# Head of a one-core transformer block: where the first transfers are issued, and a wait per pass in the first eight k tiles

## The chip, the cores and the metric

The kernel runs on one core of a Trainium2 chip. The metric is the device time of one execution in microseconds (us). Three executions of the kernel before took 547.81, 547.93 and 548.54 us: a median of 547.93.

## The reference

One layer of a hybrid streaming encoder on x of 256 tokens x 2048 features, all in float32. The part that matters here is the beginning:

```python
h = rms_norm(x, norm_gain[l])                      # x * rsqrt(mean(x*x)) * gain
proj = jnp.einsum('btd,de->bte', h, w_in[l])       # 2048 -> 9296 columns
qa, ka, va, ga, qb, kb, vb, gb, qi, ki, wi = jnp.split(proj, offsets, axis=-1)
...                                                # two attentions, gates
x = x + jnp.einsum('bte,ed->btd', y, w_out[l])     # 2048 -> 2048
return rms_norm(x, final_gain)
```

The kernel applies the gain before the matmuls and the row factor rsqrt(mean) after them, so the first projection can begin before the norm is known.

## The kernel before, in words

**The work.** Every projection is computed in column blocks of 512 with the contraction over 2048 features cut into 16 k tiles of 128. float32 accuracy is had from a faster matmul type with three passes: each operand is split into a rounded part (hi) and the rest (lo), and the product is a_hi*w_hi + a_hi*w_lo + a_lo*w_hi, each pass once per half of the 256 tokens (m = 0, 1). So one k tile of a token block is six matmuls of 512 columns. The activations are split once, at the head (acts holds a_hi and a_lo), the weights as they stream in.

**The weight stream.** A unit is two k tiles, 512 KB. Units go through a ring of four buffers (w_raw). SyncE issues the loads; ScalarE makes w_hi (a rounding copy), VectorE makes w_lo = w_raw - w_hi, TensorE multiplies. Each step tells the next by a semaphore: w_landed, hi_done, lo_done, mm_done. SyncE may load unit u when lo_done says that unit u - 4 is split.

**The head.** The first block (va, block 0 of the schedule) shares its time with the arrival of everything. Its first four units (HALVED = 4, u = 0 to 3) are loaded, split and signalled by halves of one k tile each: the first half of unit u under half_landed, half_hi and half_lo, the second under w_landed, hi_done and lo_done. The transposed activations arrive in tiles: xT tile 0 alone, tile 1 alone, then two k tiles at a time, between the weights. In this document w0a and w0b are the two halves of unit 0, w1a the first half of unit 1 (k tile 2), and so on.

- SyncE (lines 268 to 274) issues in this order: w0a, xT tile 1, w0b, xT tiles 2 and 3, w1a, w1b, xT 4 and 5, w2a, ... Units 4 to 7 (lines 275 to 280) are whole transfers, each waiting for lo_done, each followed by two xT tiles. The narrow weights (line 281) and x itself (line 286) come next on the same queue.
- ScalarE's queue issues xT tile 0 (line 663), then loads its function table (664). Its order for the halves (671 to 682) is: a_hi of k tile k (a_part, 667; for k = 1 it waits for the norm weights and for xT), then w_hi of that half (681).
- GpSimd issues the norm weights (gain, line 321: 128 rows of 64 bytes) and rel_bias (322), then fills constants.
- VectorE makes a_hi of k tile 0 itself (922), when the norm weights and xT tile 0 are there; then for each half a_lo (929), w_lo (937). Behind the eighth half it copies in bias_ext (943), which waits for rel_bias.
- TensorE first multiplies zeros (414). k tile 0 is done in three passes, each with its own wait (first_k, 417 to 428). For k tiles 1 to 7 it waits for a_lo and for w_lo, and then does all six matmuls (mm3, lines 429 to 439; mm3's own lines 371 to 373). From unit 4 on the wait is for a whole unit's lo_done (unit, 375 to 384).

After the first block, feature blocks (line 390 on, two matmuls per k tile and 128 columns), the narrow projection (447 to 451, weights nw_hi and nw_lo, split at 699 and 976), the attentions between them, and the output projection at the end.

Of the kernel before, what the change touches and what calls it, by code (L numbers as in the profile page):

```python
# [13 lines left out]
P = 128  # L14
D = 2048
T = 256
TM = T // P
KT = D // P
CB = 512
# [19 lines left out]
UK = 2  # L39
# [5 lines left out]
def hybrid_block(nc, xT, x, norm_gain, w_blocks, w_narrow, rel_bias, wo_blocks, final_gain, out):  # L45
# [7 lines left out]
    with ExitStack() as ctx:  # L53
# [11 lines left out]
        w_hi = sb("w_hi", [P, RING, UK, CB], f32r)  # L65
        w_lo = sb("w_lo", [P, RING, UK, CB], f32r)
# [5 lines left out]
        a_hi, a_lo = acts[:, :, 0, :], acts[:, :, 1, :]  # L72
# [45 lines left out]
        gain = sb("gain", [P, KT])  # L118
# [9 lines left out]
        xT_land = qk[:, :, :].rearrange("p c t -> p (c t)").rearrange("p (k t) -> p k t", k=KT)  # L128

        acc = pb("acc", [P, 4 * CB])  # L130
# [4 lines left out]
        hi_done = sem("hi_done")  # L135
# [4 lines left out]
        xT_landed = [sem(f"xT_landed{c}") for c in range(UNITS)]  # L140
# [116 lines left out]
        def _(sp):  # L257
# [9 lines left out]

            for u in range(HALVED):
                sp.dma_start(w_raw[:, u, 0:CB], w_blocks[VA_FIRST, u, :, 0:CB]).then_inc(half_landed[u], 16)
                if u == 0:  # L270
                    sp.dma_start(xT_land[:, 1, :], xT[:, 1, :]).then_inc(xT_landed[0], 16)
                sp.dma_start(w_raw[:, u, CB:2 * CB], w_blocks[VA_FIRST, u, :, CB:2 * CB]).then_inc(w_landed[u], 16)
                k = slice(UK * (u + 1), UK * (u + 2))
                sp.dma_start(xT_land[:, k, :], xT[:, k, :]).then_inc(xT_landed[u + 1], 16)
# [43 lines left out]

        @block.gpsimd
        def _(pool):  # L320
            pool.dma_start(gain[:, :], norm_gain).then_inc(gain_landed, 16)
            pool.dma_start(bias_ext[:, 0:2 * MAX_REL + 1], rel_bias).then_inc(row_landed, 16)
            nc.gpsimd.memset(ident[:, :], 0.0).then_inc(cleared, 1)
            nc.gpsimd.memset(ones[:, :], 1.0).then_inc(cleared, 1)
# [42 lines left out]
        def _(pe):  # L367
            def mm3(dst, k, m, hi, lo, start, stop):

                t = slice(m * P, m * P + P)  # L370
                nc.tensor.matmul(dst, a_hi[:, k, t], hi, start=start, stop=False)  # L371
                nc.tensor.matmul(dst, a_hi[:, k, t], lo, start=False, stop=False)  # L372
                return nc.tensor.matmul(dst, a_lo[:, k, t], hi, start=False, stop=stop)  # L373
# [40 lines left out]
                nc.tensor.matmul(acc[:, m * CB:m * CB + CB - HD // 2], ki_bd[:, 0, 0:P], zeros,  # L414
                                 start=True, stop=True)

            def first_k(a, w, start):
                for m in range(TM):
                    nc.tensor.matmul(acc[:, m * CB:m * CB + CB], a[:, 0, m * P:m * P + P], w[:, 0, 0, :],
                                     start=start, stop=False)  # L420

            pe.wait_ge(a0_done, 1)
            pe.wait_ge(half_hi, 1)
            first_k(a_hi, w_hi, True)
            pe.wait_ge(alo_done, 1)
            first_k(a_lo, w_hi, False)
            pe.wait_ge(half_lo, 1)
            first_k(a_hi, w_lo, False)
            for u in range(HALVED):
                for kk in range(UK):  # L430
                    k = u * UK + kk
                    if k == 0:
                        continue
                    pe.wait_ge(alo_done, k + 1)
                    pe.wait_ge((half_lo, lo_done)[kk], u + 1)
                    for m in range(TM):
                        last = mm3(acc[:, m * CB:m * CB + CB], k, m, w_hi[:, u, kk, :], w_lo[:, u, kk, :],
                                   False, False)
                last.then_inc(mm_done, 1)
            for u in range(HALVED, UNITS):  # L440
                pe.wait_ge(alo_done, UK * u + UK)
# [196 lines left out]
        def _(act):  # L638
# [15 lines left out]
            def features_low(g, half, first):  # L654
# [5 lines left out]
                parts = acc[:, 2 * pair * CB:2 * pair * CB + 2 * CB].rearrange("p (f x t) -> p f x t", f=2, x=2)  # L660
                nc.scalar.activation(low[:, half, :, :], parts[:, :, 1, :], ACT.Copy).then_inc(low_out, 1)  # L661

            act.dma_start(xT_land[:, 0, :], xT[:, 0, :]).then_inc(xT0_landed, 16)
            nc.scalar.preload_act_table(ACT.Exp)

            def a_part(k):
# [655 lines left out]
```

## Time and profile before

| | |
|---|---|
| runs shown, median (lowest, highest) | 547.93 us (547.81, 548.54) |
| the profiled execution's own time | 547.97 us |
| its span, first to last instruction | 546.2 us |
| mean granted clock of TensorE | 0.998 of full speed |
| TensorE busy | 535.4 us, 98% |
| VectorE busy | 332.0 us, 61% |
| ScalarE busy | 259.3 us, 47% |
| GpSimd busy | 17.1 us, 3% |
| moved by DMA | 103.73 MB, mean 190 GB/s |

The profile comes from one execution. Its span lies inside the execution's own time. Engines are PE (TensorE matmuls), PEld (its weight loads), DVE (VectorE), ACT (ScalarE), POOL (GpSimd) and SP (SyncE); a q behind the name is the sequencer that issues transfers. A busy share is an average over the whole span: where the time can change is read from idle stretches of the engine that ends last and from what ended them.

### The profile page before, as it was taken

The numbers are of one execution on the slowest core, as the hardware profiler recorded it, in microseconds if no ns is written. First come the engines' busy times: TensorE is split into PE (matmuls) and PEld (weight loads), VectorE is DVE, ScalarE is ACT, GpSimd is POOL, SyncE is SP. The second block draws the span as 40 slices with busy tenths as digits, with TensorE's granted clock in tenths as the row PEclk, the third lists the DMA queues.
The fourth block names the chain that finished last, engine by engine and source line by source line (L and its number), as shares of the span: only waits on it lengthen the run. The fifth ranks groups of instructions, "written<-read, shape, count | busy, mean of one in ns | idle before, by whom it ended". The sixth has DMA issues, their size and how long they took to land.

```text
span 546.2 us, 8107 instructions
## 1 busy us (share of the span) xinstructions
PE 535.4 (98%) x2780; PEld 454.7 (83%) x2780; DVE 332.0 (61%) x488; ACT 259.3 (47%) x364; POOL 17.1 (3%) x31
## 2 busy tenths in 40 slices
PE   7999999999999999999999999999999999999994
PEld 4889888888888888888888888888888888888883
DVE  5855564656566565567655657556674757556464
ACT  6883544444444443444554545354445445444342
POOL 1002020202000000000000000000000000000000
PEclk9999999999999999999999999999999999999999
DMA  8987655557555656665555554554555566565613
GB/s 289 394 290 241 189 168 182 168 170 237 185 174 174 199 193 189 191 193 162 181 160 167 173 157 158 184 164 157 181 168 172 159 218 217 188 199 184 211 57 154
DMA packets 59909, 103.73 MB, mean 190 GB/s; under 512 B 3280, under 2 KB 44656, under 8 KB 59376
## 3 DMA queue, kind: packets, MB, share of 16 engines
q1 hardware_dynamic: 58944, 98.78, 55.5%
q0 software_dynamic: 656, 4.22, 2.4%
q10 hardware_dynamic: 288, 0.46, 0.2%
q8 instruction: 12, 0.20, 0.2%
q14 instruction: 9, 0.07, 0.0%
HBM read 101.34 MB, written 2.11 MB: 189 GB/s over the span
## 4 chain that ended last, share of the span: by engine, by line
PE 97%; DMA 1%; DVE 1%; ACT 0%; SPq 0%; issue 0%; DVEq 0%; ACTq 0%
PE acc L404 27%; PE acc L371 16%; PE acc L373 16%; PE acc L372 16%; PE acc L402 13%; PE aux L546 1%; PE aux L522 1%; DMA w_raw<-w_blocks 1%; PE aux L449 1%; PE aux L484 1%; PE acc L407 1%; PE aux L550 1%; PE aux L525 1%; PE aux L535 1%; PE aux L486 1%; PE aux L605 0%
## 5 line engine op out<-in xcount | busy, mean ns | idle before, releaser
L896 DVE TENSOR_TENSOR w_lo<-w_raw,w_hi 128x1024 fp32r<-128x1024 f32 x172 | 212.3, 1236 | 187.4 <-ACT w_hi L646 186.8
L646 ACT ACTIVATE w_hi<-w_raw 128x1024 fp32r<-128x1024 f32 x172 | 182.0, 1059 | 242.5 <-PE acc L404 123.3
L404 PE MATMUL acc<-acts,w_hi 128*128 128x512 f32 x640 | 224.3, 396 | 0.0
L402 PE MATMUL acc<-acts,w_lo 128*128 128x256 f32 x600 | 168.8, 281 | 0.0
L371 PE MATMUL acc<-w_hi,acts 128*128 128x512 f32 x382 | 150.5, 394 | 1.8 <-DVE w_lo L937 1.5
L373 PE MATMUL acc<-w_hi,acts 128*128 128x512 f32 x382 | 149.0, 390 | 0.0
L372 PE MATMUL acc<-w_lo,acts 128*128 128x512 f32 x382 | 148.7, 389 | 0.0
L404 PEld LDWEIGHTS acc<-acts,w_hi 128*128 128x128 f32 x640 | 119.1, 188 | 26.1
L402 PEld LDWEIGHTS acc<-acts,w_lo 128*128 128x128 f32 x600 | 113.1, 189 | 0.8
L371 PEld LDWEIGHTS acc<-w_hi,acts 128*128 128x128 f32 x382 | 71.8, 188 | 17.1 <-issue 2.8
L373 PEld LDWEIGHTS acc<-w_hi,acts 128*128 128x128 f32 x382 | 71.7, 188 | 15.2
L372 PEld LDWEIGHTS acc<-w_lo,acts 128*128 128x128 f32 x382 | 71.8, 188 | 14.4
L860 ACT ACTIVATE t_gate<-z 128x512 f32<-128x512 f32 x8 | 5.0, 627 | 15.3 <-DVE z L1246 15.3
L661 ACT ACTIVATE low<-acc 128x512 f32<-128x512 f32 x20 | 11.6, 581 | 0.0
L407 PE MATMUL acc<-acts,w_lo 128*128 128x256 f32 x40 | 11.2, 281 | 0.0
L1027 DVE SCALAR_TENSOR_TENSOR iscore<-relu,w_idx,iscore 128x256 f32<-128x256 f32 (+1 forms) x32 | 11.2, 413 | 0.0
L910 DVE TENSOR_TENSOR qk<-acc,low 128x512 f32<-128x512 f32 (+1 forms) x16 | 10.9, 684 | 0.0
L363 POOL DMA_DIRECT2D v<-x x1 | 0.5, 531 | 317.7 <-PE aux L550 317.7
L840 ACT ACTIVATE acts<-aux 128x512 fp32r<-128x512 f32 x8 | 4.7, 605 | 9.4 <-PE aux L605 9.4
L777 ACT ACTIVATE p<-p,neg_top,q_rate 128x256 f32<-128x256 f32 (+1 forms) x16 | 8.5, 535 | 1.0 <-DVE neg_top L1130 1.0
L546 PEld LDWEIGHTS aux<-v,pT 128*128 128x128 f32 x64 | 8.4, 191 | 0.5
L546 PE MATMUL aux<-v,pT 128*128 (+1 forms) x64 | 8.4, 275 | 0.0
(137 smaller groups left out, 306.9 us busy)
## 6 DMA issues: line engine op xcount, KB each, us to landing
w_raw<-w_blocks SPq DMA_DIRECT2D x140, 512.0 KB, 3.6
w_raw<-wo_blocks SPq DMA_DIRECT2D x32, 512.0 KB, 3.4
w_raw<-w_blocks SPq DMA_DIRECT2D x8, 256.0 KB, 6.3
v<-x SPq DMA_DIRECT2D x2, 1024.0 KB, 9.4
v<-x POOLq DMA_DIRECT2D x1, 2048.0 KB, 8.7
qk<-xT SPq DMA_DIRECT2D x7, 256.0 KB, 6.5
o<-ext_dram POOLq DMA_DIRECT2D x1, 1024.0 KB, 6.9
fgain<-final_gain POOLq DMA_DIRECT2D x1, 1024.0 KB, 7.5
```

The costliest lines, as they stand in the source:

```text
L371: nc.tensor.matmul(dst, a_hi[:, k, t], hi, start=start, stop=False)
L372: nc.tensor.matmul(dst, a_hi[:, k, t], lo, start=False, stop=False)
L373: return nc.tensor.matmul(dst, a_lo[:, k, t], hi, start=False, stop=stop)
L402: nc.tensor.matmul(acc[:, bank:bank + T], w_lo4[:, u % RING, q, c], a_hi[:, k, :], start=False, stop=False)
L404: last = nc.tensor.matmul(whole, w_hi4[:, u % RING, q, c], acts[:, k, :, :], start=(k == 0), stop=(k == KT - 1))
L407: nc.tensor.matmul(acc[:, bank:bank + T], w_lo4[:, u % RING, q, c], a_hi[:, k, :], start=False, stop=False)
L546: nc.tensor.matmul(aux[3][:, h * HD:h * HD + HD], pT1[:, h, kt, :], v_flat[:, ds(place(pair, kt) + h * HD, HD)], start=(kt == 0), stop=(kt ...
L646: nc.scalar.activation(flat(w_hi[:, s, :, :]), w_raw[:, s, :], ACT.Copy).then_inc(hi_done, 1)
L661: nc.scalar.activation(low[:, half, :, :], parts[:, :, 1, :], ACT.Copy).then_inc(low_out, 1)
L896: nc.vector.tensor_tensor(flat(w_lo[:, s, :, :]), w_raw[:, s, :], flat(w_hi[:, s, :, :]).bitcast(f32), ALU.subtract).then_inc(lo_done, 1)
L910: nc.vector.tensor_tensor(dst, parts[:, :, 0, :], low[:, half, :, :], ALU.add).then_inc(feat_out, 1)
L1027: last = nc.vector.scalar_tensor_tensor(total[:, :], relu[:, h, :], w_idx[:, 1 - t, 4 * i + 2 * c + h:4 * i + 2 * c + h + 1], total[:, :], ...
```

## The change

It moves three issues and cuts one wait. xT tile 1 goes from SyncE's queue to ScalarE's, the norm weights from GpSimd's to ScalarE's; ScalarE then issues norm weights, xT tile 0, xT tile 1, in this order, ahead of its table load. On SyncE w0a and w0b are then the first two. In the first eight k tiles TensorE does three passes per k tile in the order a_hi*w_hi, a_lo*w_hi, a_hi*w_lo, with a wait before each: for w_hi and a_hi, for a_lo, for w_lo. first_k is replaced by early_pass; the number of matmuls is the same. Units 4 to 7 and everything behind them stay.

```diff
--- before.py
+++ after.py
@@ -267,8 +267,6 @@
 
             for u in range(HALVED):
                 sp.dma_start(w_raw[:, u, 0:CB], w_blocks[VA_FIRST, u, :, 0:CB]).then_inc(half_landed[u], 16)
-                if u == 0:
-                    sp.dma_start(xT_land[:, 1, :], xT[:, 1, :]).then_inc(xT_landed[0], 16)
                 sp.dma_start(w_raw[:, u, CB:2 * CB], w_blocks[VA_FIRST, u, :, CB:2 * CB]).then_inc(w_landed[u], 16)
                 k = slice(UK * (u + 1), UK * (u + 2))
                 sp.dma_start(xT_land[:, k, :], xT[:, k, :]).then_inc(xT_landed[u + 1], 16)
@@ -318,7 +316,6 @@
 
         @block.gpsimd
         def _(pool):
-            pool.dma_start(gain[:, :], norm_gain).then_inc(gain_landed, 16)
             pool.dma_start(bias_ext[:, 0:2 * MAX_REL + 1], rel_bias).then_inc(row_landed, 16)
             nc.gpsimd.memset(ident[:, :], 0.0).then_inc(cleared, 1)
             nc.gpsimd.memset(ones[:, :], 1.0).then_inc(cleared, 1)
@@ -414,28 +411,25 @@
                 nc.tensor.matmul(acc[:, m * CB:m * CB + CB - HD // 2], ki_bd[:, 0, 0:P], zeros,
                                  start=True, stop=True)
 
-            def first_k(a, w, start):
+            def early_pass(a, w, k, start=False):
                 for m in range(TM):
-                    nc.tensor.matmul(acc[:, m * CB:m * CB + CB], a[:, 0, m * P:m * P + P], w[:, 0, 0, :],
-                                     start=start, stop=False)
-
-            pe.wait_ge(a0_done, 1)
-            pe.wait_ge(half_hi, 1)
-            first_k(a_hi, w_hi, True)
-            pe.wait_ge(alo_done, 1)
-            first_k(a_lo, w_hi, False)
-            pe.wait_ge(half_lo, 1)
-            first_k(a_hi, w_lo, False)
+                    last = nc.tensor.matmul(acc[:, m * CB:m * CB + CB], a[:, k, m * P:m * P + P],
+                                            w[:, k // UK, k % UK, :], start=start, stop=False)
+                return last
+
             for u in range(HALVED):
                 for kk in range(UK):
                     k = u * UK + kk
+                    pe.wait_ge((half_hi, hi_done)[kk], u + 1)
                     if k == 0:
-                        continue
+                        pe.wait_ge(a0_done, 1)
+                    else:
+                        pe.wait_ge(ahi_done, k)
+                    early_pass(a_hi, w_hi, k, start=(k == 0))
                     pe.wait_ge(alo_done, k + 1)
+                    early_pass(a_lo, w_hi, k)
                     pe.wait_ge((half_lo, lo_done)[kk], u + 1)
-                    for m in range(TM):
-                        last = mm3(acc[:, m * CB:m * CB + CB], k, m, w_hi[:, u, kk, :], w_lo[:, u, kk, :],
-                                   False, False)
+                    last = early_pass(a_hi, w_lo, k)
                 last.then_inc(mm_done, 1)
             for u in range(HALVED, UNITS):
                 pe.wait_ge(alo_done, UK * u + UK)
@@ -660,7 +654,9 @@
                 parts = acc[:, 2 * pair * CB:2 * pair * CB + 2 * CB].rearrange("p (f x t) -> p f x t", f=2, x=2)
                 nc.scalar.activation(low[:, half, :, :], parts[:, :, 1, :], ACT.Copy).then_inc(low_out, 1)
 
+            act.dma_start(gain[:, :], norm_gain).then_inc(gain_landed, 16)
             act.dma_start(xT_land[:, 0, :], xT[:, 0, :]).then_inc(xT0_landed, 16)
+            act.dma_start(xT_land[:, 1, :], xT[:, 1, :]).then_inc(xT_landed[0], 16)
             nc.scalar.preload_act_table(ACT.Exp)
 
             def a_part(k):
```

## Rows read from the trace of the kernel before

**Rows 1.** the page: TensorE's busy line, and the chain's shares by engine

```profile
PE 535.4 (98%) x2780; PEld 454.7 (83%) x2780; DVE 332.0 (61%) x488; ACT 259.3 (47%) x364; POOL 17.1 (3%) x31
...
PE 97%; DMA 1%; DVE 1%; ACT 0%; SPq 0%; issue 0%; DVEq 0%; ACTq 0%
```

**Rows 2.** timeline of TensorE: start us, us, instruction [idle before <-releaser]

```profile
8.10 0.47 PE L371 MATMUL acc<-w_hi,acts 128*128 128x512 f32 x1 [1.12 <-DVE w_lo L937]
...
10.08 0.47 PE L371 MATMUL acc<-w_hi,acts 128*128 128x512 f32 x1 [0.35 <-DVE w_lo L937]
...
11.09 0.39 PE L372 MATMUL acc<-w_lo,acts 128*128 128x512 f32 x1
...
449.71 0.47 PE L371 MATMUL acc<-w_hi,acts 128*128 128x512 f32 x1 [0.36 <-DVE acts L1227]
```

**Rows 3.** windows: us, busy (x) of each engine, clock, DMA share, GB/s

```profile
12.00:538.90 526.90, 526.54 (x2757) 450.02 (x2755) 322.96 (x470) 250.64 (x349) 14.41 (x12) 1.00 0.58 188
```

**Rows 4.** the chain that ended last, up to k tile 2: start, us, what

```profile
2.61 5.94 DMA w_raw<-w_blocks
8.58 0.64 ACT w_hi L681
9.24 0.70 DVE w_lo L937
```

**Rows 5.** timeline of VectorE, k tiles 2 and 3

```profile
8.49 0.48 DVE L929 SCALAR_TENSOR_TENSOR acts<-qk,gain,acts 128x256 fp32r<-128x256 f32 x1 [0.54 <-ACT acts L667]
...
10.25 0.68 DVE L937 TENSOR_TENSOR w_lo<-w_raw,w_hi 128x512 fp32r<-128x512 f32 x1
```

**Rows 6.** DMA issues of the first 2 us: KB each, us to landing

```profile
qk<-xT ACTq DMA_DIRECT2D x1, 128.0 KB, 3.6
```

**Rows 7.** timeline of the head: issues, table load, first halves

```profile
0.75 0.42 ACTq L663 DMA_DIRECT2D qk<-xT  x1
...
1.20 0.42 SPq L271 DMA_DIRECT2D qk<-xT  x1
1.20 1.28 ACT L664 ACT_TABLE_LOAD   x1 [1.20 <-PEq L1315]
1.25 0.68 POOL L321 DMA_DIRECT2D gain<-norm_gain  x1 [0.79 <-POOLq L1315]
...
4.20 0.63 ACT L681 ACTIVATE w_hi<-w_raw 128x512 fp32r<-128x512 f32 x1 [1.72 <-DMA w_raw<-w_blocks]
...
4.72 0.35 DVE L922 TENSOR_SCALAR acts<-qk,gain 128x256 fp32r<-128x256 f32 x1 [3.31 <-DMA gain<-norm_gain]
```

**Rows 8.** windows from 4 to 10, columns as in rows 3

```profile
4.00:6.00 2.00, 1.69 (x6) 0.60 (x4) 1.24 (x3) 1.03 (x2) 0.00 (x0) 1.00 0.85 242
6.00:8.00 2.00, 0.98 (x4) 0.30 (x2) 1.29 (x3) 0.68 (x2) 0.00 (x0) 1.00 0.98 318
8.00:10.00 2.00, 1.63 (x6) 1.05 (x6) 1.24 (x3) 1.88 (x4) 0.00 (x0) 1.00 1.05 402
```

**Rows 9.** timeline around unit 4

```profile
15.28 1.06 ACT L646 ACTIVATE w_hi<-w_raw 128x1024 fp32r<-128x1024 f32 x1 [0.29 <-DMA w_raw<-w_blocks]
...
16.37 1.23 DVE L896 TENSOR_TENSOR w_lo<-w_raw,w_hi 128x1024 fp32r<-128x1024 f32 x1 [0.47 <-ACT w_hi L646]
...
18.36 0.39 PE L371 MATMUL acc<-w_hi,acts 128*128 128x512 f32 x1
```

**Rows 10.** timeline around the narrow weights

```profile
37.85 1.47 DVE L976 TENSOR_TENSOR nw_lo<-nw_raw,nw_hi 128x1280 fp32r<-128x1280 f32 x1
...
40.52 0.40 PE L449 MATMUL aux<-acts,nw_hi 128*80 128x256 f32 x2
```

**Rows 11.** DMA queues over 0 to 40 us: packets, MB, share

```profile
q10 hardware_dynamic: 144, 0.13, 0.9%
q0 software_dynamic: 96, 0.03, 0.4%
```

**Rows 12.** window behind the last matmul, columns as in rows 3

```profile
542.00:544.00 2.00, 0.00 (x0) 0.00 (x0) 0.23 (x1) 0.00 (x0) 0.00 (x0) 1.00 0.83 313
```

## The prediction

> **What bounds the kernel now.** I read the page first. TensorE is busy 98% of the 546.2 us span, and 97% of the chain that ended last is TensorE [rows 1]. Nothing in the diff removes a matmul, so the change can only shorten time in which TensorE stands still, and only at the head, where the diff works. TensorE's own timeline shows how much there is [rows 2]: it has 1.12 us of idle before k tile 1 (8.10) and 0.35 before k tile 2 (10.08). Behind that it is busy in 526.5 of the 526.9 us from 12 to 538.9 [rows 3]; the one gap, 0.36 at 449.71, waits for VectorE's y tiles, which TensorE itself feeds, so it moves with the rest [rows 2]. The only number that can move the end is therefore the time at which the unbroken run of matmuls begins, 10.08, provided that what comes after can keep up with an earlier start.
>
> The chain that ended last says what sets 10.08 [rows 4]: the first half of the second weight unit (w1a) is issued on SyncE at 2.61 and its landing comes 5.94 us later, at 8.55; ScalarE rounds it to w_hi (8.58 to 9.21), VectorE makes w_lo (9.24 to 9.93), and TensorE starts 0.15 us later. Its activations are there before: a_lo, made from a_hi, starts at 8.49 and ends at 8.97 [rows 5]. The 5.94 us are not latency of one transfer. The first xT tile, issued at 0.75 to empty engines, took 3.6 us [rows 6]. The DMA engines are 85, 98 and 105% busy in the stretches from 4 to 10 [rows 8], so w1a waits for the bytes ahead of it.
>
> **The change part by part.** *A wait per pass* (eight k tiles). Before, k tile 2 waited for a_lo and w_lo, then ran six matmuls. Now its first two, a_hi with w_hi, need only w_hi (9.21) and a_hi. With the same 0.15 us from an operand's end to the matmul, they start at 9.36, 0.72 earlier. The fifth matmul of a k tile starts 1.01 after its first (11.09 against 10.08 [rows 2]), so the third pass is due at 10.37; w_lo is usable at 9.93 + 0.15 = 10.08, so the third pass finds it ready and there is no new gap. For later k tiles TensorE needs 1.38 us each ((18.36 - 10.08) / 6, [rows 2, 9]), while VectorE starts the next w_lo 1.01 after this one (9.24, 10.25 [rows 4, 5]), so the cover grows. The extra waits (three per k tile for two) stand in TensorE's sequencer, ahead of the array: free here, since the run has matmuls queued. If that cover went, the price would be 0.15 for one. Same matmuls, another order: their price stays at 1.38 / 6 = 0.23.
>
> *What is late next.* Unit 4, the first with whole 512 KB transfers, keeps the old wait. Its weights reach ScalarE at 15.28 (that engine was idle 0.29 for the DMA), w_lo starts at 16.37 and ends at 17.60, so TensorE can start at 17.75 at the earliest; it starts at 18.36 now [rows 9]. The slack is 0.61, under the 0.72. So of the 0.72 only 0.61 gets through, the rest becomes a 0.1 us gap at unit 4. Units 5 to 7 gain cover: VectorE needs 2 x 0.48 + 1.23 = 2.19 for a unit [rows 5, 9], TensorE 2 x 1.38. The next tight place is the narrow weights: their w_lo ends at 37.85 + 1.47 = 39.32 and TensorE takes it up at 40.52, a slack of 1.05 with the 0.15 off [rows 10], more than 0.61. So k tiles 2 to 7 and unit 4 both go by the DMA stream, and every shift of that stream, D, moves both: gain = min(0.72, 0.61) - D.
>
> *k tile 1, both halves first on SyncE.* The 128 KB xT tile leaves SyncE's queue, so every later issue there is one issue slot, 0.47 us, earlier (SyncE's second issue is at 1.20, its fifth at 2.61: [rows 4, 7]). Its w0b now lands between 4.8 (its new issue at 1.20 plus 3.6) and, if nothing is won, 1.5 us before k tile 1's start at 8.10, that is 6.6 (0.63 for w_hi, 0.69 for w_lo and the hand-over). Either way its w_hi is there by 7.3 and k tile 1 is over by 8.8, before 9.36. It is off the path: the 1.12 us of idle shrinks and the idle before k tile 2 grows by as much. For w1a the 0.47 is worth nothing as long as the DMA engines are full: the same bytes stand ahead of it (two weight halves, xT0 and xT1 with 128 KB each, now both on ScalarE's queue, and the double tile of k 2 and 3). Were ScalarE's queue served beside SyncE's with engines of its own, w1a would land up to 0.47 earlier and the sum would be 547.0. The Trainium skill, page "DMA: Bandwidth & Descriptors", section "Issuing engines are not separate DMA queues", says that all issuers share the same 16 engines and only issue time is saved; by that rule the term is zero, and the full engines agree.
>
> *ScalarE's queue and norm weights.* ScalarE now issues three transfers instead of one: 2 x 0.42 us more before its table load (1.28 long, [rows 7]), so that ends at 3.3 instead of 2.48. The first w_hi starts at 4.20, so 0.9 of cover is left. Were it gone, only k tile 0 would move, which is off the path. xT0 is issued 0.45 later and lands about 4.8 rather than 4.35; the norm weights leave at 0.75 instead of 1.25 and land before the 4.72 that they set now; a_hi of k tile 0 comes within 0.2 of the present 4.72 [rows 6, 7]. xT1, behind xT0 and beside w0b, lands at 5 to 5.6 instead of 4.7; ScalarE needs it before w_hi of k tile 1: off the path. GpSimd loses 0.68 us of issue and sends rel_bias that much sooner; what uses it comes on VectorE behind the eighth w_lo half, which the chain has not reached by 10.25, so nothing waits for it.
>
> *Price of the small packets.* The norm weights are 128 rows of 64 B. No row shows such rows on a hardware queue. On GpSimd's queue the whole head's 96 small packets took 0.4% of 16 x 40 us, 27 ns each; on ScalarE's queue 144 packets (128 of 1 KB and 16 completion writes) took 0.9%, 40 ns each [rows 11]. With their 16 completion writes the new rows cost 144 x 27 = 3.9 us over 16 engines = 0.24 us, less 0.05 for the 32 packets that leave GpSimd's queue: +0.19. The ends are 0 (they are issued first of all, when the engines have nothing else) and 0.36 (40 ns). I take 0.19, by the row of small packets. The Trainium skill, page "DMA: Bandwidth & Descriptors", section "Why small descriptors are slow (HBM only)", charges a fixed overhead per packet, which points the same way; no row here shows it for 64 B.
>
> *The shortfall.* From 4 to 8 the engines moved 242 and 318 GB/s, from 8 to 10 402, though busy [rows 8]. The lacking 0.49 MB are 1.2 us at 402. GpSimd's queue sends its two small transfers in these microseconds; whether it is the cause can't be read. If the shortfall goes, D falls by 1.2; if it doubles, D rises by 1.2. I take it as it is, since most of its bytes come after the moved pieces.
>
> **Sum.** D = +0.19, gain 0.61 - 0.19 = 0.42. The profiled execution took 547.97 (span 546.2 and 1.8 around it), 0.04 over the median of 547.93: 547.97 - 0.42 = 547.55, called 547.5. About 0.2% (1.1 us) is what a measurement can tell from no change.
>
> **The rivals.**
> - *The shortfall vanishes* (faster). For it: it ends soon after GpSimd's two small transfers, and one of them is taken off that queue. Against: low rates last to 7, and rel_bias stays there. Gives 547.5 - 1.2 = 546.3, or 546.9 if half goes. Chance 0.18 for enough of it to pass the 0.2%.
> - *The clock falls in the new idle* (slower). k tile 1 may be over at 7.7 to 8.8 with k tile 2 at 9.36: one idle stretch of up to 1.6 us, where 1.12 and 0.35 stood. If TensorE went to 1.2 GHz there, each k tile would take 1.38 more; between one and two tiles long, this costs some 2 us: 549.5. It decides as soon as it takes more than 0.42, two matmuls' worth. Against: the granted clock is 1.00 through the idle of before (6 to 10, [rows 8]), and after the last matmul, with no work for TensorE from 539 on, the window 542 to 544 still has 1.00 [rows 12]. Chance 0.04.
> - *The shortfall deepens*, two hardware queues taking turns for longer: D = +1.2 more, 548.7 at full size, slower than before from D = 0.61. Chance 0.10, of which 0.04 beyond the 0.2%.
> - *Nothing changes*: w_hi and a_hi aren't what ends last, or unit 4 gives all back: 547.9. Chance 0.08.
> - My forecast: 0.60, own range 547.1 to 547.9.
>
> Faster by over 0.2%: 0.18. Slower: 0.08. Within: 0.74. The range leaves out the full clock case and the last of the vanished shortfall: 546.4 to 548.4.
>
> **What would show it.** In the timeline of the changed kernel k tile 2's first pass starts right behind its w_hi, at about 9.4 to 9.6; the unbroken run starts there; ScalarE's wait for unit 4 is at 15.3 to 15.5, and a TensorE gap of about 0.1 stands at 17.8 to 18.0; the granted clock stays 1.00. The windows 4 to 8 keep their 240 and 320 GB/s. I am wrong if w1a's w_hi starts before 8.1 or after 9.3, if unit 4's moves by over 0.5, or if TensorE shows a new gap behind 20.

## The result and the profile after

The changed kernel takes 548.54 us (median of 22 runs, 547.61 to 550.37), the kernel before 547.72 in the same comparison (22 runs, 547.17 to 548.65). The ratio is 1.0018, 95% interval 1.0011 to 1.0024: slower by some 0.8 us, little, but the interval is clear of 1. The forecast was 547.5 in a range of 546.4 to 548.4: wrong in sign, and the time lies just outside. Ratios and intervals, here and below, are taken over the executions and are not quotients of the two medians printed beside them; they leave out two executions that lie far off, 1094.31 us of the kernel before and 670.88 of e3's.

The profiled execution took 548.76, with a span of 547.0. Of the changed kernel's page, the lines that answer to [rows 1] and the line of ScalarE's queue:

```profile
PE 536.9 (98%) x2780; PEld 456.3 (83%) x2780; DVE 331.6 (61%) x488; ACT 259.1 (47%) x364; POOL 16.6 (3%) x30
...
q10 hardware_dynamic: 576, 0.60, 0.3%
...
PE 97%; DMA 1%; ACT 0%; DVE 0%; ACTq 0%; issue 0%; DVEq 0%
```

The same matmuls are busy 1.5 us longer than before (536.9 against 535.4): a first hint that some ran slower. From 12 us on nothing has changed. This window answers to [rows 3]: TensorE again lacks 0.36 us in the whole stretch.

```profile
12.00:539.70 527.70, 527.34 (x2761) 450.62 (x2759) 323.18 (x471) 250.99 (x349) 14.46 (x12) 1.00 0.57 188
```

So the loss is at the head. The timeline of the changed kernel there (start us, us, instruction, idle before and what ended it), beside [rows 2, 4, 5, 7]; line 416 is the new early_pass, x4 and x2 are merged matmuls:

```profile
5.10 0.35 DVE L918 TENSOR_SCALAR acts<-qk,gain 128x256 fp32r<-128x256 f32 x1 [3.68 <-DMA qk<-xT]
...
5.60 2.05 PE L416 MATMUL acc<-w_hi,acts 128*128 128x512 f32 x4 [0.77 <-DVE acts L918]
...
7.65 0.51 ACT L663 ACTIVATE acts<-qk,gain 128x256 fp32r<-128x256 f32 x1 [3.22 <-DMA qk<-xT]
8.07 0.61 ACT L677 ACTIVATE w_hi<-w_raw 128x512 fp32r<-128x512 f32 x1
...
8.73 1.94 PE L416 MATMUL acc<-w_hi,acts 128*128 128x512 f32 x4 [0.24 <-ACT w_hi L677]
...
10.52 0.63 PE L416 MATMUL acc<-w_lo,acts 128*128 128x512 f32 x2
...
10.98 1.08 PE L416 MATMUL acc<-w_hi,acts 128*128 128x512 f32 x4
...
12.36 0.84 PE L416 MATMUL acc<-w_hi,acts 128*128 128x512 f32 x3
```

Two things are to be seen. First, ScalarE stands idle for 3.22 us until xT tile 1 has landed, and only then makes a_hi and w_hi of k tile 1, so that TensorE starts k tile 1 at 8.73 instead of 8.10. Second, its first four matmuls take 1.94 us; k tile 2's take 1.08. They are 0.43 apart, twice the 0.23 of the rest: TensorE ran at the lower of its two levels, 1.2 GHz, until about 10.4. The chain that ended last starts with the same transfer, where before it started with w1a:

```profile
0.75 0.42 ACTq L657
1.21 0.45 ACTq L658
1.68 5.88 DMA qk<-xT
7.65 0.51 ACT acts L663
8.16 0.53 ACT w_hi L677
8.73 10.58 PE acc L416 x42
```

The windows of the DMA engines, as in [rows 8]:

```profile
4.00:6.00 2.00, 1.23 (x3) 0.43 (x2) 0.87 (x3) 0.43 (x1) 0.00 (x0) 1.00 0.92 206
6.00:8.00 2.00, 2.00 (x6) 1.39 (x5) 0.57 (x1) 0.35 (x1) 0.00 (x0) 1.00 1.04 351
8.00:10.00 2.00, 1.76 (x5) 1.07 (x4) 1.77 (x4) 2.00 (x6) 0.00 (x0) 1.00 1.06 408
```

The low rate is still there, a little earlier. The clock column reads 1.00 here, although the matmuls in it are 0.43 apart: ahead of the first change that a profile records, this column says nothing. It was one of my arguments against the clock.

Of the signs that the prediction named for being wrong, none came: w1a's w_hi started at 8.99, unit 4's at 14.92 (0.36 earlier), and no gap stands behind 20. What did show it is the first pass of k tile 2, at 10.98 and not at 9.4 to 9.6.

### The profile page after: what moved, and what is told of

Same layout as the page of the kernel before. It is cut to its first block, busy times and chain, and to the rows that moved or that the text cites. A ratio compares the mean times of both kernels' runs of the same rounds, so it can differ in the third digit from the quotient of the medians.

```text
span 547.0 us, 8107 instructions
## 1 busy us (share of the span) xinstructions
PE 536.9 (98%) x2780; PEld 456.3 (83%) x2780; DVE 331.6 (61%) x488; ACT 259.1 (47%) x364; POOL 16.6 (3%) x30
## 4 chain that ended last, share of the span: by engine, by line
PE 97%; DMA 1%; ACT 0%; DVE 0%; ACTq 0%; issue 0%; DVEq 0%
PE acc L401 27%; PE acc L368 15%; PE acc L370 15%; PE acc L369 15%; PE acc L399 13%; PE acc L416 2%; PE aux L540 1%; PE aux L516 1%; DMA qk<-xT 1%; PE aux L443 1%; PE aux L478 1%; PE acc L404 1%; PE aux L544 1%; PE aux L519 1%; PE aux L529 1%; PE aux L480 1%
## 5 line engine op out<-in xcount | busy, mean ns | idle before, releaser
L369 PE MATMUL acc<-w_lo,acts 128*128 128x512 f32 x368 | 143.2, 389 | 0.0
L370 PEld LDWEIGHTS acc<-w_hi,acts 128*128 128x128 f32 x368 | 69.1, 188 | 14.8
L368 PEld LDWEIGHTS acc<-w_hi,acts 128*128 128x128 f32 x368 | 69.1, 188 | 14.3 <-issue 0.6
L369 PEld LDWEIGHTS acc<-w_lo,acts 128*128 128x128 f32 x368 | 69.1, 188 | 13.8
L416 PE MATMUL acc<-w_hi,acts 128*128 128x512 f32 x32 | 10.4, 455 | 1.0 <-DVE acts L918 0.8
L416 PEld LDWEIGHTS acc<-w_hi,acts 128*128 128x128 f32 x32 | 6.8, 221 | 4.4 <-issue 2.1
```

Of the source, the lines that this page charges most:

```text
L416: last = nc.tensor.matmul(acc[:, m * CB:m * CB + CB], a[:, k, m * P:m * P + P], w[:, k // UK, k % UK, :], start=start, stop=False)
```

## The experiments

Three theories: Q, the transfer order (xT1 is late and ScalarE takes its a_hi ahead of w_hi); C, the clock; and, as a rival, that waits or passes themselves cost something. Kernels measured together share their runs of the kernel before, so its median differs a little below (547.40 to 547.65).

### e1 and e1b: the waits per pass alone

All transfers as before; in TensorE's program first_k and the loop behind it are replaced:

```diff
-            def first_k(a, w, start):
+            def early_pass(a, w, k, start=False):
...
-                    for m in range(TM):
-                        last = mm3(acc[:, m * CB:m * CB + CB], k, m, w_hi[:, u, kk, :], w_lo[:, u, kk, :],
-                                   False, False)
+                    last = early_pass(a_hi, w_lo, k)
```

> The kernel before with the three waits per k tile alone; all transfers are issued as before. Theory Q (the loss comes from the transfer order: xT tile 1 on ScalarE's queue lands at 7.56 instead of 4.5, and ScalarE takes its a_hi ahead of w_hi of k tile 1): no loss here, k tile 2 starts behind its w_hi at 9.4, time 0.3 to 0.6 us under the kernel before. Theory C (the loss comes from TensorE's clock, which the changed kernel's profile shows at its lower level until 10.40 and the old one's at its upper level from 4.72): the same here if the rise needs what TensorE does before 5.1, since that is unchanged; so also no loss. Theory W (the waits themselves or the new order of passes cost something): slower than before by 0.3 or more.

> The kernel of e1 once more, on the same chip as e14, to compare the two and to settle whether the waits per pass alone are faster than the kernel before: 0.2 to 0.5 us under it, at the floor of 547.2 in most executions; its trace has the narrow matmuls 0.2 to 0.4 us behind the end of their w_lo.

Measured: 547.32 against 547.64 (ratio 0.9998, 0.9989 to 1.0007), and again 547.12 against 547.54 (0.9997, 0.9987 to 1.0006). The medians are 0.3 and 0.4 lower, but both intervals hold 1: the waits do no harm, and their gain can't be told from none. Theory W falls. The trace of e1b shows a head much faster than that of [rows 2], and where the gain goes (timeline):

```profile
7.50 1.07 PE L419 MATMUL acc<-w_hi,acts 128*128 128x512 f32 x4
...
8.86 1.07 PE L419 MATMUL acc<-w_hi,acts 128*128 128x512 f32 x4
...
10.22 1.07 PE L419 MATMUL acc<-w_hi,acts 128*128 128x512 f32 x4
...
36.20 0.40 PE L404 MATMUL acc<-acts,w_hi 128*128 128x512 f32 x1
36.80 0.39 PE L402 MATMUL acc<-acts,w_lo 128*128 128x256 f32 x1 [0.21 <-DVE w_lo L893]
...
39.49 0.39 PE L404 MATMUL acc<-acts,w_hi 128*128 128x512 f32 x1
39.73 0.40 PE L446 MATMUL aux<-acts,nw_hi 128*80 128x256 f32 x2
```

k tile 3 starts at 10.22; in the trace of [rows 2] it starts at 11.54, 1.32 later. The same two feature matmuls in the trace of the kernel before:

```profile
37.46 0.40 PE L404 MATMUL acc<-acts,w_hi 128*128 128x512 f32 x1
37.69 0.28 PE L402 MATMUL acc<-acts,w_lo 128*128 128x256 f32 x1
```

So e1b is still 1.26 ahead at 36.20 (37.46 before), and 0.89 at 36.80, where TensorE waits for the w_lo of a feature unit; the first matmuls behind the wait cost another 0.1. The narrow matmuls then start at 39.73, 0.79 earlier than in [rows 10]. They follow the end of their own w_lo (37.98 + 1.47 = 39.45) by 0.28, as expected, but they did not wait for it: they start 0.24 behind the matmul at 39.49, the ordinary distance. The chain of e1b says what holds that feature unit (start, us, what):

```profile
21.22 11.30 DMA v<-x
...
34.54 0.96 ACT w_hi L643
35.53 1.24 DVE w_lo L893
...
36.80 0.39 PE acc L402
```

It is x itself, 11.3 us on its way. ScalarE squares each half of x for the norm (1.9 us) before it makes w_hi of this unit, so everything behind waits for x to land. In the trace of e1 the same place takes its lead from 0.96 to 0.77.

### e2: the moved transfers alone

The changed kernel with TensorE's old waits.

> The changed kernel with the old waits of TensorE (six matmuls of a k tile behind a_lo and w_lo): the three moved transfers alone. Theory Q: k tile 1 has to wait for w_lo, about 9.4 + 0.15 = 9.55, instead of w_hi, 8.73; k tile 2 follows at 10.9 at the upper clock against 10.08 before: 0.8 us slower than the kernel before, even with the clock up, and about as slow as or slower than the changed kernel. Theory C: slower only by what the lower clock takes, 0.8 to 2 us, and the profile shows matmuls 0.43 us apart at 8 to 10.

Measured: 551.53 (550.79 to 551.69) against 547.64, ratio 1.0064 (1.0051 to 1.0078): 3.9 us slower, more than either theory said. xT tiles on ScalarE's queue took 5.5 us at the median; its k tile 1 starts at

```profile
10.61 0.77 PE L368 MATMUL acc<-w_hi,acts 128*128 128x512 f32 x1 [2.00 <-DVE w_lo L936]
...
11.17 0.63 PE L369 MATMUL acc<-w_lo,acts 128*128 128x512 f32 x1
...
11.60 0.63 PE L370 MATMUL acc<-w_hi,acts 128*128 128x512 f32 x1
```

after 2.0 us of idle, with matmuls 0.43 apart. So the transfers are the harmful half of the change, and the waits per pass buy some 3 us of it back. How much of these 3 us is the clock can't be told from one trace: in it xT1 landed later (8.6) than in any trace of the changed kernel, and matmuls stayed 0.43 apart until 14.2.

### e3: xT tile 1 back on SyncE's queue

```diff
                 sp.dma_start(w_raw[:, u, 0:CB], w_blocks[VA_FIRST, u, :, 0:CB]).then_inc(half_landed[u], 16)
+                if u == 0:
+                    sp.dma_start(xT_land[:, 1, :], xT[:, 1, :]).then_inc(xT_landed[0], 16)
...
-            act.dma_start(xT_land[:, 1, :], xT[:, 1, :]).then_inc(xT_landed[0], 16)
```

> The changed kernel with xT tile 1 back on SyncE's queue behind the first half weights; norm weights and xT tile 0 stay on ScalarE's queue, the waits per pass stay. Theory Q: xT1 lands at 4.5 to 5 again, k tile 1 starts at 6.5 to 7.3, k tile 2 behind its w_hi at 9.0 to 9.4: 0.5 to 1 us faster than the kernel before. Theory C: k tile 0 still starts late (xT0 behind the norm weights, 5.5 instead of 5.1), the clock stays low until past 8 in most executions, but since the run of matmuls begins with k tile 2 at 9.4 the lower clock costs only what is left of it: between 0.5 faster and 0.5 slower than the kernel before.

Measured: 547.64 against 547.64, ratio 0.9997 (0.9987 to 1.0006). With the one moved issue put back, the loss is gone. Its trace has xT1 landing 3.4 us after its issue; k tile 1 starts at 7.77, 2 at 9.27, 3 at 10.67. The 0.5 to 1 us under the kernel before that theory Q promised did not come; the time lies in theory C's range, but the late clock that C expected isn't in the trace either (the first four matmuls of k tile 0 take 1.17). This execution took 548.25: 0.7 ahead of the kernel before until 36 us, it lost 1.0 in a gap at 37.92, at the same feature unit as in e1b, where x landed at 33.6 and not 32.5.

### e6 and e10: what stands ahead on ScalarE's queue

e6 has the norm weights back on GpSimd's queue, e10 issues them last. e10's edit:

```diff
-            act.dma_start(gain[:, :], norm_gain).then_inc(gain_landed, 16)
             act.dma_start(xT_land[:, 0, :], xT[:, 0, :]).then_inc(xT0_landed, 16)
             act.dma_start(xT_land[:, 1, :], xT[:, 1, :]).then_inc(xT_landed[0], 16)
+            act.dma_start(gain[:, :], norm_gain).then_inc(gain_landed, 16)
```

> The changed kernel with the norm weights back on GpSimd's queue; xT tiles 0 and 1 stay on ScalarE's. Theory G (the 128 small rows ahead of xT0 and xT1 cost ScalarE's queue a turn each, beside a 2 KB packet of SyncE's queue): xT0 lands near 4.3 again and xT1 0.7 or more earlier than 7.56; the time falls by 0.5 us or more against the changed kernel. Theory X (xT1 is late because it stands on a second queue, behind xT0 and beside the bytes of SyncE's queue while the rate is low from 4 to 7): xT1 lands at 6.8 or later all the same, ScalarE's w_hi of k tile 1 starts at 7.4 or later, and the time stays within 0.4 us of the changed kernel.

> The changed kernel with ScalarE's three transfers in the order xT0, xT1, norm weights. Theory G (xT1 is late because it stands behind the 128 small rows): xT0 lands near 4.4, xT1 near 5.4 as in e6, and now it is the norm weights that are late, 5.5 to 7; k tile 0 then starts at 6 or later, k tile 1's w_hi at 7.4 to 8.1, and the time stays between the kernel before and the changed one. Theory X2 (ScalarE's queue as such is served late): xT1 lands at 6.8 or later in this order too, and the time is the changed kernel's or above.

Measured: e6 548.24 against 547.65 (1.0004, 0.9994 to 1.0013); e10 549.63 against 547.40 (1.0044, 1.0031 to 1.0057). DMA issues of the first 2 us, e6 and then e10 (KB each, median us to landing):

```profile
qk<-xT ACTq DMA_DIRECT2D x2, 128.0 KB, 3.9
...
gain<-norm_gain POOLq DMA_DIRECT2D x1, 8.0 KB, 4.3
```

```profile
qk<-xT ACTq DMA_DIRECT2D x2, 128.0 KB, 3.9
...
gain<-norm_gain ACTq DMA_DIRECT2D x1, 8.0 KB, 5.2
```

With nothing ahead, both xT tiles land in time (xT1 at 5.4 in both); X and X2 fall. The loss of e6 can't be told from none, though its median is 0.6 above: in its trace k tile 0 waits for the norm weights until 5.6 and runs at the lower clock. But G isn't shown either: e6 gained 0.3 on the changed kernel and not 0.5, e10 is slower than the changed kernel, and in e10 the norm weights, 8 KB, take 5.2 us as third transfer, where xT1, 128 KB, took 5.9 as third in the changed kernel. What they share is the slot, issued at 1.68, and what stands beside it: SyncE's third transfer, the 256 KB of xT 2 and 3, issued 0.01 earlier. In the changed kernel's list of issues it took 5.7 us:

```profile
qk<-xT SPq DMA_DIRECT2D x1, 256.0 KB, 5.7
```

and landed at 7.38, xT1 at 7.56; in e10 it landed at 6.69, the norm weights at 6.90. Whether the small rows ahead add to xT1's delay is left open. e10 also loses because k tile 0 waits for the norm weights, 2.77 us of idle, and in its trace the clock falls to 0.50 at 7.76 and comes back at 11.17.

### e4, e8, e13: filling TensorE's idle

The changed kernel with more zero matmuls, before k tile 0 (e4; e8 is the same for a second trace), and in e13 between k tiles 0 and 1 as well. e13's edit (e4 has the first line only):

```diff
+            nc.tensor.matmul(acc[:, 0:192], ki_bd[:, 0, 0:P], zeros[:, 0:192], start=True, stop=True)
...
+                    if k == 0:
+                        for m in (0, 1, 0):
+                            nc.tensor.matmul(acc[:, m * CB:m * CB + 192], ki_bd[:, 0, 0:P], zeros[:, 0:192],
+                                             start=False, stop=False)
```

> The changed kernel with one more zero matmul of 192 columns ahead of the first pass, so that TensorE works until about 5.5 and has next to no idle before k tile 0. Nothing else is touched. Theory C (the clock rises late because TensorE stands idle before a later first pass): the clock is up by 7 in the profile, the matmuls of k tile 1 are 0.23 apart, and the time falls by 0.8 us, to that of the kernel before. Theory Q alone: no change against the changed kernel, 0.8 us slower than before. Both together: the time equals the kernel before, as k tile 2 would start at 8.73 + 1.4 = 10.1 with the clock up, just where it stood.

> The same kernel as e4, for a second trace: its times lay at 547.9 and 549.0 but also three times at 550.3 to 550.6, while the one trace, of an execution of 547.91, shows the upper clock from 4.35 on. Theory C2 (the clock rises during the zero matmuls and falls again in the idle of 1.5 us between k tiles 0 and 1, or rises only late): in a slow execution matmuls of k tiles 1 to 3 are 0.43 apart. Theory D (the slow executions come from late transfers): matmuls are 0.23 apart throughout and xT1 or unit 4 lands 2 us later.

> The changed kernel with the longer zero matmuls of e4 and three more zero matmuls of 192 columns between k tiles 0 and 1 (they add zero to the sums), so that TensorE has next to no idle from 1.5 to 8.7 while all transfers are as in the changed kernel. Theory C (what the changed kernel loses beyond the kernel before is TensorE's clock, low for longer because TensorE stands idle before k tile 0 and before k tile 1): the time is 547.4 to 548.0, 0.5 or more under the changed kernel, no execution at 550, and the trace shows the clock up before 8.2 and staying. Theory Q alone (the transfers set it, whatever the clock): within 0.3 of the changed kernel's 548.5 or above.

Measured: e4 550.32 (547.91 to 550.63) against 547.64, ratio 1.0042 (1.0028 to 1.0056); e8's one execution 547.98; e13 548.96 (548.35 to 550.02) against 547.40, ratio 1.0033 (1.0021 to 1.0046). Both traces of e4's kernel have the upper clock from k tile 0 on, start k tile 1 at 8.71 and 8.67 and take 547.91 and 547.98, as expected where transfers and a good clock act together. They are the cleanest pair with the changed kernel's first trace, which starts k tile 1 at the same 8.73 with the lower clock and took 548.76. But the median of e4 is 1.8 above the changed kernel's, which none of the theories expected: the longer zero matmuls are no cure. Its executions of 550.3 to 550.6 have a mean granted clock of 0.992 to 0.994 where that of 547.91 has 0.998, which speaks for C2, a fall in mid-course; I have no trace of one. e13 went against theory C and as theory Q alone says: no time came back. Its trace has the upper clock from 4.8 on and is slow by the transfer alone; xT1 landed at 8.1:

```profile
9.27 1.19 PE L417 MATMUL acc<-w_hi,acts 128*128 128x512 f32 x4 [0.87 <-ACT w_hi L682]
...
10.76 1.09 PE L417 MATMUL acc<-w_hi,acts 128*128 128x512 f32 x4
...
12.14 1.07 PE L417 MATMUL acc<-w_hi,acts 128*128 128x512 f32 x4
```

### e9, e15, e16: three more traces of the changed kernel

> The changed kernel again, for a second trace. If xT1's landing on ScalarE's queue is what holds k tile 1, it lands between 6.8 and 8.6 here too and k tile 1 starts 1.1 us behind it; the time is then 547.6 to 550.4, by the clock in the first 12 us. If the 7.56 of the first trace was chance, it lands before 6 and the time is below 547.6.

> The changed kernel, a third trace. Theory C (clock beside transfers): its time follows from two rows, the start of k tile 1 (8.2 to 8.8, by xT1's landing at 7.0 to 7.6) and the clock: with the upper clock by 8, 547.4 to 548.0; with the lower clock until 10 or later, 548.6 or more. Transfers alone: the time follows k tile 1's start, whatever the clock.

> The changed kernel, a fourth trace; the same expectation as for the third.

Measured, one execution each: 547.51, 549.46 and 550.71. TensorE's timeline of e9, k tiles 1 and 3:

```profile
8.24 1.20 PE L416 MATMUL acc<-w_hi,acts 128*128 128x512 f32 x4 [1.18 <-ACT w_hi L677]
...
11.10 1.07 PE L416 MATMUL acc<-w_hi,acts 128*128 128x512 f32 x4
```

of e15:

```profile
6.84 1.16 PE L416 MATMUL acc<-w_hi,acts 128*128 128x512 f32 x4 [2.02 <-DVE acts L918]
...
8.91 2.08 PE L416 MATMUL acc<-w_hi,acts 128*128 128x512 f32 x4 [0.19 <-ACT w_hi L677]
...
13.08 1.07 PE L416 MATMUL acc<-w_hi,acts 128*128 128x512 f32 x4
```

with its windows (columns as in [rows 3]; the clock is the third number from the end):

```profile
5.00:8.34 3.34, 1.50 (x6) 0.90 (x6) 1.44 (x3) 0.51 (x2) 0.00 (x0) 1.00 0.96 326
8.34:11.75 3.41, 3.22 (x9) 2.26 (x8) 3.35 (x7) 3.41 (x8) 0.00 (x0) 0.50 1.05 399
11.75:14.00 2.25, 2.25 (x12) 1.84 (x11) 2.25 (x6) 2.25 (x6) 0.00 (x0) 1.00 1.05 403
```

and of e16:

```profile
9.63 2.07 PE L416 MATMUL acc<-w_hi,acts 128*128 128x512 f32 x4 [1.36 <-ACT w_hi L677]
...
12.36 1.66 PE L416 MATMUL acc<-w_hi,acts 128*128 128x512 f32 x4
...
14.32 1.08 PE L416 MATMUL acc<-w_hi,acts 128*128 128x512 f32 x4
```

In e15 xT0 landed late too (at 6.2, issued at 1.20), TensorE stood idle for 2.02 us before k tile 0, and the clock, up when k tile 0 ran (four matmuls in 1.16), fell to the lower level for the next microseconds. In e16 it was low until 13.6. xT1 landed at 7.74 and 8.47, and k tile 1 started later than the expectation had it. Both theories act, and they add up. Take e9 as base (k tile 1 at 8.24, k tile 3 at 11.10, 2.86 apart at the upper clock) and shift its time by the start of k tile 3, that is, 536.41 plus that start:

| trace | k tile 1 | k tile 3 | apart | 536.41 + k tile 3 | took |
|---|---|---|---|---|---|
| before | 8.10 | 11.54 | 3.44 | 547.95 | 547.97 |
| changed, first | 8.73 | 12.36 | 3.63 | 548.77 | 548.76 |
| changed, e9 | 8.24 | 11.10 | 2.86 | (base) | 547.51 |
| changed, e15 | 8.91 | 13.08 | 4.17 | 549.49 | 549.46 |
| changed, e16 | 9.63 | 14.32 | 4.69 | 550.73 | 550.71 |
| e13 | 9.27 | 12.14 | 2.87 | 548.55 | 548.55 |
| e10 | 9.82 | 13.22 | 3.40 | 549.63 | 549.65 |
| e1b | 7.50 | 10.22 | 2.72 | 546.63 | 547.13 |

All but e1b agree within 0.03 us; e1b is 0.5 above, which is what the feature unit behind x took back at 36.80. In the changed kernel's four traces xT1 moves k tile 1 by up to 1.39 (8.24 to 9.63), and the clock adds 0, 0.77, 1.31 and 1.83 to the distance of k tiles 1 and 3. (Before, the distance holds 0.35 of idle that the old wait left.)

The lower clock during k tile 0 is not the changed kernel's own. With the transfers as before the first four matmuls of k tile 0 took 2.05 us in e1, 2.00 in e1b and 2.04 in e11. There k tile 1 follows without idle, at 7.50 to 7.70, and its four take 1.07 to 1.09, at the upper clock. In the changed kernel's first trace and in e16 TensorE then stood idle for 0.24 and 1.36 us, waiting for xT1's tile, and the clock stayed low until 10.4 and 13.6.

### e7: rel_bias late

e1's kernel with GpSimd's remaining small transfer moved behind a wait:

```diff
-            pool.dma_start(bias_ext[:, 0:2 * MAX_REL + 1], rel_bias).then_inc(row_landed, 16)
...
+            pool.wait_ge(hi_done, 1)
+            pool.dma_start(bias_ext[:, 0:2 * MAX_REL + 1], rel_bias).then_inc(row_landed, 16)
```

> The kernel of e1 (the kernel before with the waits per pass) with rel_bias issued on GpSimd only behind the second w_hi half (about 7.5) instead of at 1.9. Theory B (GpSimd's transfer of 8 rows of 1028 bytes slows the DMA engines from 4 to 7): the windows 4 to 8 move 350 GB/s and more, w1a's w_hi starts by 8.0, unit 4's w_hi by 14.4, and the time is 0.3 us or more under e1's. Theory N (the low rate has nothing to do with that transfer): windows 4 to 8 stay at 240 to 330 GB/s, and the time is e1's within 0.2 us.

Measured: 547.40 against 547.65, ratio 0.9995 (0.9986 to 1.0003), e1's time. Windows 4 to 8 of e7:

```profile
4.00:6.00 2.00, 1.55 (x4) 0.67 (x3) 1.20 (x3) 1.69 (x3) 0.00 (x0) 1.00 0.92 290
6.00:8.00 2.00, 2.00 (x11) 1.60 (x10) 1.72 (x4) 1.17 (x3) 0.53 (x1) 1.00 0.90 316
```

Theory N: 290 and 316 GB/s, and e1's time. w1a's w_hi did start at 7.34, as theory B has it, but the rate stayed low and unit 4's w_hi started at 15.24. rel_bias isn't the cause of the low rate, and what is stays open.

### e11, e12, e14: looking for a better version

e11 gives units 4 to 7 the same treatment as the head; e12 adds the norm weights on ScalarE's queue behind xT0; e14 is e11 with VectorE's nw_lo ahead of rk_cols and q_unit.

```diff
-                pe.wait_ge(alo_done, UK * u + UK)
-                unit(0, u)
+                pe.wait_ge(hi_done, u + 1)
+                pe.wait_ge(alo_done, UK * u + UK)
+                for part, (a, w) in enumerate(((a_hi, w_hi), (a_lo, w_hi), (a_hi, w_lo))):
+                    if part == 2:
+                        pe.wait_ge(lo_done, u + 1)
...
```

> The kernel of e1 (transfers as before, waits per pass in k tiles 0 to 7) with units 4 to 7 of the first block treated alike: both w_hi passes of a unit behind hi_done, the w_lo pass behind lo_done. Theory U (unit 4's wait for w_lo is the wall that gives the gain of e1 back: its TensorE start is 0.15 behind the end of w_lo in the traces of e1 and e3): unit 4 starts right behind k tile 7 or 0.15 behind w_hi's end, and the time falls by a further 0.3 to 1.0 us, until the next wall. Theory L (a later place, the narrow weights or units 8 to 11 that wait for x, sets the floor of 547.0 to 547.2 that all faster kernels share): the time stays e1's within 0.2 us.

> The kernel of e11 with the norm weights on ScalarE's queue behind xT0, and xT1 on SyncE's queue as before. If the norm weights' way over GpSimd's queue (landing at 4.6 to 5.6 in the traces) costs anything, k tile 0 starts at 4.9 to 5.1 steadily and the clock is up earlier more often: 0 to 0.4 us under e11. If the small rows beside the first weight halves cost more than that, 0.2 or more above e11.

> The kernel of e11 with VectorE's nw_lo (1.47 us) moved ahead of rk_cols and q_unit, which nothing needs before 57 us. Theory L (the faster kernels share a floor because the narrow weights' w_lo ends at 39.3 to 39.5 in all of them and TensorE starts on it 0.27 behind): nw_lo ends near 38.9, the narrow matmuls start at 39.2, and the time is 0.3 to 0.5 us under e11 and e1, so 546.8 to 547.1. If the head alone (the first 18 us) set the time: as e11, 547.3 to 547.5.

Measured: e11 547.47 against 547.40 (1.0000, 0.9991 to 1.0008), e12 547.70 against 547.40 (1.0004, 0.9995 to 1.0013), e14 547.53 against 547.54 (0.9998, 0.9990 to 1.0007). None differs from the kernel before by more than the measurement can tell. For e11 theory L holds, with the second of its two places, the units that wait for x: unit 4 starts at 17.23, right behind k tile 7, but a lead of 1.13 over the kernel before at 36.33 is 0.78 at 37.03, behind the same feature unit as in e1b, and the narrow matmuls start at 39.74 like e1's two. e12 is 0.2 above e11, within the noise; k tile 0 started at 5.36 and its clock was up only at 9.1, so the steadier start did not come. e14 is a miss, and it shows that the narrow weights are not the wall: nw_lo ends at 38.76, 0.7 earlier, and the time does not follow. TensorE has its gap (0.44) at 36.57, at the feature unit behind x, and the lead falls there from 1.73 to 1.02. Its traced execution took 546.94, its median is no better. Not tried is w_hi of that unit ahead of ScalarE's square of x.

## Why the prediction was wrong

**Right.** The head moves the end: each microsecond by which the unbroken run starts later goes into the time, and one by which it starts earlier does so until the next wall. The waits per pass do what was worked out: in e1b k tile 2 starts at 8.86, 0.33 behind the end of its w_hi and ahead of its w_lo, without idle. The wall at unit 4 is where it was put: e1 and e3 start it 0.15 behind w_lo. e1's medians lie 0.3 and 0.4 under the kernel before, against 0.6 without the small packets, though not beyond their intervals.

**The step that failed** is xT1's landing "at 5 to 5.6 instead of 4.7", called "off the path", and with it k tile 1, which was to be "over by 8.8" and off the path too. xT1 lands at 7.56, and at 7.1 to 8.5 in the other traces of the changed kernel (chains of e9 and e16); k tile 1 starts at 8.73. I took little more than the 3.3 to 3.6 us of transfers issued by 1.25 for one issued at 1.68, although the profile before had a warning: w0b, issued at 1.67, landed only at 6.6. It was no fixed price, since w0b in that slot took 3.6 us in e7 and e11 and 5.4 in e3; but xT1, third on ScalarE's queue, took 5.4 us or more in every trace that has it there. The change swaps the two. Before, the later of xT1 and w0b was w0b with 6.6; after, it is xT1 with 7.56, a microsecond later. ScalarE makes a_hi before w_hi, so another 0.5 us comes on top, and w_hi of k tile 1 starts at 8.07 instead of 6.60. Behind it ScalarE's order holds k tile 2, although w1a is there. e3 and e6 show it: with that one issue put back, or with xT1 second on ScalarE's queue, the ratio to the kernel before is 0.9997 and 1.0004, and both intervals hold 1 (e6's reaches 1.0013, so it says less).

**The second** is the clock, which I had as a rival at 0.04, priced 549.5. In three of the four traces of the changed kernel it cost 0.8 to 1.8 us: in two it was still low while k tile 1 ran, in e15 it fell at 8.34, behind 2.0 us of idle and most of k tile 0. At the upper clock the first trace's k tile 1 at 8.73 would have given 536.41 + 8.73 + 2.86 = 548.0, the time of the kernel before: the late tile ate what the waits win, and the clock made the slowdown. That is read from traces; the two kernels that were to keep the clock up, e4 and e13, gave no time back at the median, so how much of the median's 0.8 is the clock stays open. That e15 took 549.46, almost the price I had named, is luck: 1.3 of it is the clock, where I had 2, and the rest is xT1. My argument, that it holds for microseconds behind the last matmul [rows 12], was true and did not carry over; the other, the column's 1.00 at the head, was no evidence.

**A wall that was missed.** The prediction took the narrow weights, slack 1.05, for the next tight place behind unit 4. The feature unit behind x was tighter: in the kernel before its w_lo ends at 36.61 and TensorE takes it up at 37.69, a slack of 0.93 with the 0.15 off:

```profile
35.39 1.22 DVE L896 TENSOR_TENSOR w_lo<-w_raw,w_hi 128x1024 fp32r<-128x1024 f32 x1 [2.88 <-ACT w_hi L646]
```

The forecast gain of 0.42 would not have met it; the leads of e1 (0.96) and e1b (1.26) did.

**Sizes.** D was to be +0.19. w1a's landing was complete at 8.07 instead of 8.55 in the first trace of the changed kernel, and unit 4's w_hi started at 14.92 instead of 15.28. But this is no size of D: with the transfers as before w1a landed at 7.86 in e1 and 7.88 in e1b, and in the changed kernel at 7.51 in e9 and 8.68 in e16. Against this spread neither the small packets' 0.19 nor SyncE's issue slot of 0.47 can be read. The Trainium skill's rule ("DMA: Bandwidth & Descriptors", section "Issuing engines are not separate DMA queues") that only issue time is saved is neither borne out nor contradicted by it.

## What to carry to other kernels

When transfers are reordered at the head, price each by its issue slot, look up what stood in that slot before and how much its landing varies, then ask which of a tile's inputs now lands last; moving one forward may only change which one is late. In such a head an idle microsecond of TensorE can be paid twice, by its own length and by the clock. A matmul that starts shortly behind an operand did not have to wait for it: look for the gap in TensorE's own row. Ahead of a profile's first recorded clock change the distance between matmuls tells the clock, the column does not; and one trace of an effect this small is one draw: the four of the same kernel lay 3.2 us apart.

## What the runs showed that was not expected

- An 8 KB transfer took 5.2 us in the third slot of ScalarE's queue (e10) and 3.2 in the first (the changed kernel). Transfers that SyncE and ScalarE issued from 1.20 on landed, in every trace here, in the order of their issue across both queues: xT 2 and 3 (SyncE, 1.67), xT1 (ScalarE, 1.68) and w1a (SyncE, 2.14) at 7.38, 7.56 and 8.07 in the changed kernel's first trace and at 7.74, 8.47 and 8.68 in e16.
- TensorE's clock fell again at 8.34 in e15 and at 7.76 in e10, behind 2.02 and 2.77 us of idle before k tile 0 and some of k tile 0's matmuls, and was up again at 11.75 and 11.17; over the 1.5 us of idle in e4 and e8's traces, and the 1.1 of [rows 2], it held.
- The low DMA rate between 4 and 7 us is there with both of GpSimd's small transfers in it (before, e1), with rel_bias alone (the changed kernel) and with the norm weights alone (e7).
